# The down-projection of an MLP by quarters: seven block products in place of eight, with the block sums on GpSimd

## The reference

```python
def squared_relu_mlp(h, w_up, w_down):
    a = jax.nn.relu(h @ w_up)
    return (a * a) @ w_down

for layer in range(DEPTH):
    ...
    hn = rmsnorm(x, g[2])
    x = x + rmsnorm(squared_relu_mlp(hn, w_mlp_up[layer], w_mlp_down[layer]), g[3])
```

## Time and profile before

| | |
|---|---|
| median of 3 runs | 1166.92 us (1164.58 to 1167.45) |
| the profiled execution | 1166.92 us, its span 1165.1 us |
| mean granted TensorE clock | 0.985 of full speed |
| PE busy | 1116.0 us (96%) |
| DVE busy | 600.7 us (52%) |
| ACT busy | 450.2 us (39%) |
| POOL busy | 192.3 us (17%) |

### The profile page before, as it was taken

How to read it: one execution, slowest core, us unless ns; L and a number is a source line. 1 busy time by engine, 2 the same in 40 slices (tenths; PEclk the granted TensorE clock), 3 DMA queues, 4 the chain that set the end, 5 groups by cost and what they waited for, 6 DMA issues and landing times. The chain is left out here.

```text
span 1165.1 us, 15098 instructions
## 1 busy us (share of the span) xinstructions
PE 1116.0 (96%) x5577; PEld 896.5 (77%) x5577; DVE 600.7 (52%) x1106; ACT 450.2 (39%) x854; POOL 192.3 (17%) x338
## 2 busy tenths in 40 slices
PE   7999999999999999999899787999999999999997
PEld 6776678988888888888667665658988888888885
DVE  4353544543543643647377976634553453553554
ACT  6376554241321321335354366553332322322322
POOL 1354520000000000005303268340000000000004
PEclk9999899999999999999999889999999999999999
DMA  7431403354444344442423314003353543443431
GB/s 220 91 73 37 109 1 73 73 126 94 90 107 98 84 107 100 84 106 56 113 42 73 72 37 109 1 1 73 73 125 75 109 108 74 107 108 76 105 73 72
DMA packets 50782, 97.71 MB, mean 84 GB/s; under 512 B 4448, under 2 KB 4640, under 8 KB 50720
## 3 DMA queue, kind: packets, MB, share of 16 engines
q1 hardware_dynamic: 50208, 96.78, 36.5%
q10 hardware_dynamic: 512, 0.11, 0.1%
HBM read 94.78 MB, written 2.10 MB: 83 GB/s over the span
## 5 line engine op out<-in xcount | busy, mean ns | idle before, releaser
L1789 PE MATMUL bank<-w_hi,r_hi 128*128 128x512 f32 x512 | 199.3, 389 | 0.0
L1791 PE MATMUL bank<-w_hi,r_lo 128*128 128x512 f32 x512 | 199.2, 389 | 0.0
L1790 PE MATMUL bank<-w_lo,r_hi 128*128 128x512 f32 x512 | 199.2, 389 | 0.0
L1013 DVE SCALAR_TENSOR_TENSOR w_lo<-w_raw,gT,w_hi 128x512 fp32r<-128x512 f32 x152 | 104.5, 751 | 149.3 <-ACT w_hi L678 149.2
L1468 PE MATMUL bank<-r_hi,w_hi 128*128 128x512 f32 (+1 forms) x456 | 177.5, 389 | 0.0
L1469 PE MATMUL bank<-r_hi,w_lo 128*128 128x512 f32 (+1 forms) x456 | 177.4, 389 | 0.0
L1470 PE MATMUL bank<-r_lo,w_hi 128*128 128x512 f32 (+1 forms) x456 | 177.4, 389 | 0.0
L678 ACT ACTIVATE w_hi<-w_raw,gT 128x512 fp32r<-128x512 f32 x152 | 97.1, 713 | 174.7 <-PE bank L1791 103.7
L1003 DVE TENSOR_TENSOR w_lo<-w_raw,w_hi 128x2048 fp32r<-128x2048 f32 x34 | 78.3, 2302 | 124.7 <-ACT w_hi L670 124.7
L670 ACT ACTIVATE w_hi<-w_raw 128x2048 fp32r<-128x2048 f32 x36 | 68.9, 1913 | 157.5 <-PE bank L1791 118.7
L1790 PEld LDWEIGHTS bank<-w_lo,r_hi 128*128 128x128 f32 x512 | 96.1, 188 | 20.1
(11 more groups left out here) (169 smaller groups left out, 1664.7 us busy)
## 6 DMA issues: line engine op xcount, KB each, us to landing
w_raw<-in_w_mlp_up SPq DMA_DIRECT2D x64, 512.0 KB, 6.0
w_raw<-in_w_mlp_down SPq DMA_DIRECT2D x64, 512.0 KB, 6.4
w_raw<-in_b_w_in SPq DMA_DIRECT2D x16, 512.0 KB, 6.3
w_raw<-in_a_w_in SPq DMA_DIRECT2D x8, 512.0 KB, 6.7
w_raw<-in_a_w_out SPq DMA_DIRECT2D x8, 512.0 KB, 5.6
w_raw<-in_b_w_out SPq DMA_DIRECT2D x8, 512.0 KB, 5.9
X<-in_x SPq DMA_DIRECT2D x4, 512.0 KB, 6.7
w_raw<-in_a_w_in SPq DMA_DIRECT2D x8, 256.0 KB, 7.2
```

The lines of the kernel that those rows point to most:

```text
L1013: last = nc.vector.scalar_tensor_tensor(out=w_l[:, cs], in0=w_raw[:, slot, cs], scalar=g, in1=w_h[:, cs].bitcast(f32), op0=ALU.mult, op1=A ...
L1789: nc.tensor.matmul(bank[:], xh, hi[:, k, :], start=h == 0 and k == 0, stop=False)
L1790: nc.tensor.matmul(bank[:], xh, lo[:, k, :], start=False, stop=False)
L1791: ins = nc.tensor.matmul(bank[:], xl, hi[:, k, :], start=False, stop=h == 1 and k == 3)
```

## The change

Within a quarter the hidden activations A (512 tokens x 1024) and the down weights B (1024 x 1024) are cut into 2 x 2 blocks, A into blocks of 256 tokens x 512, B into blocks of 512 x 512. Seven products of Winograd's form of Strassen's method take the place of eight:

S1 = A21 + A22, S2 = S1 - A11, S3 = A11 - A21, S4 = A12 - S2; T1 = B12 - B11, T2 = B22 - T1, T3 = B22 - B12, T4 = T2 - B21.

They are numbered 0 to 6 in the order in which PE does them: A11 B11, S1 T1, S2 T2, S4 B22, A12 B21, S3 T3, A22 T4. Each is two token blocks x four hidden blocks x three matmuls, 24 matmuls of 512 columns. The products of the four quarters are added up each in an accumulator of its own (`acc`, seven of 2 x 512 a partition, read from the banks by DVE, `taken`), and only in the last quarter are the accumulators combined into the four blocks of y: six sums of 1024 on POOL (`total`), one on DVE, and the last two reads of banks go into y's blocks directly.

The eight sums of blocks S and T are made on POOL, each in two halves of 512 (S) or 1024 (T) numbers a partition, and written over blocks no longer needed. Up weights and B blocks now share four places for raw weights. High and low parts of the seven pairs are made in halves, on ACT (`a_high`, `b_high`) and DVE (`a_low`, `b_low`). ReLU is now on ACT (`relu_tile`), the square a product of ReLU and bank on DVE (`squared`). A product's weights take the two places of `w_hi` and `w_lo` in turn, so a place is free for product i when product i - 2 has left it. The quarters are written out in place of loops.

```diff
+PRODUCTS = (("A11", "B11"), ("S1", "T1"), ("S2", "T2"), ("S4", "B22"), ("A12", "B21"), ("S3", "T3"), ("A22", "T4"))
...
         @block.sync
...
+                for q in range(QUARTERS):
+                    u = u0 + MLP_UNITS * q
+                    if q == 0:
+                        for n in range(UPS):
+                            load(u + n, up_source(0, n))
+                        sp.wait_ge(x_new, 8 * (2 * layer + 1))
+                    else:
+
+                        sp.wait_ge(b_lo_done, part_no(layer, q - 1, 3, 1))
+                        sp.wait_ge(t_made, t_no(layer, q - 1, "T2", 1))
+                        fetch(u, up_source(q, 0))
...
+                        sp.wait_ge(*low_of(u))
+                    fetch((layer, q, "B22"), down_source(q, "B22"))
+                    sp.wait_ge(*low_of(u + (1 if q else 2)))
+                    fetch((layer, q, "B12"), down_source(q, "B12"))
+                    sp.wait_ge(*low_of(u + 3))
+                    fetch((layer, q, "B11"), down_source(q, "B11"))
+                    sp.wait_ge(b_lo_done, part_no(layer, q, 1, 1))
+                    sp.wait_ge(t_made, t_no(layer, q, "T2", 1))
+                    fetch((layer, q, "B21"), down_source(q, "B21"))
...
+            def weight_sum(layer, q, name, a):
...
+                elif name == "T1":
+                    pool.wait_ge(*loaded((layer, q, "B11")))
+                    pool.wait_ge(t_made, t_no(layer, q, "T3", a))
+                    nc.gpsimd.tensor_tensor(of("T1"), of("B12"), of("B11"), ALU.subtract).then_inc(t_made, 1)
+                elif name == "T2":
+                    pool.wait_ge(t_made, t_no(layer, q, "T1", a))
+                    pool.wait_ge(b_lo_done, part_no(layer, q, 0, a))
+                    nc.gpsimd.tensor_tensor(of("T2"), of("B22"), of("T1"), ALU.subtract).then_inc(t_made, 1)
...
+            def mlp(layer):
+                norm = 2 * layer + 2
+                for q in range(QUARTERS):
+                    last = q == QUARTERS - 1
+                    for a in range(2):
+                        weight_sum(layer, q, "T3", a)
+                    for a in range(2):
+                        hidden_sum(layer, q, "S3", a)
+                    for name in ("T1", "T2"):
+                        for a in range(2):
+                            weight_sum(layer, q, name, a)
+                    for name in ("S1", "S2", "S4"):
+                        for a in range(2):
+                            hidden_sum(layer, q, name, a)
+                    if last:
+                        pool.wait_ge(tile_out, part_tile(layer, q, 0, 1) + 1)
+                        total(layer, 2, 0, ALU.add)
+                        total(layer, 4, 0, ALU.add)
+                        pool.wait_ge(tile_out, part_tile(layer, q, 1, 1) + 1)
+                        total(layer, 3, 1, ALU.add)
+                    for a in range(2):
+                        weight_sum(layer, q, "T4", a)
+                pool.wait_ge(tile_out, part_tile(layer, QUARTERS - 1, 2, 1) + 1)
+                total(layer, 5, 2, ALU.add)
+                pool.wait_ge(acc_g, 6 * layer + 4)
+                total(layer, 1, 5, ALU.add)
+                total(layer, 6, 5, ALU.subtract)
+                gained(norm, 0, 1)
+                gained(norm, 1, 1)
...
         @block.vector
...
+            def a_low(layer, q, i, a):
+                hi, lo = (v[:, 2 * a:2 * a + 2, :] for v in hid[layer][A_PLACE[i]])
+                dve.wait_ge(a_hi_done, part_no(layer, q, i, a))
+                nc.vector.tensor_tensor(lo, a_of(PRODUCTS[i][0], a), hi.bitcast(f32), ALU.subtract).then_inc(a_lo_done, 1)
...
+                for q in range(QUARTERS):
...
+                    for i in range(2, PARTS):
+                        b_low(layer, q, i, 0)
+                        for j in range(2):
+                            taken(layer, q, i - 2, j)
+                        if last and i == 4:
+                            dve.wait_ge(acc_g, 6 * layer + 3)
+                            dve.wait_ge(tile_out, part_tile(layer, q, 2, 1) + 1)
+                            nc.vector.tensor_tensor(acc[:, 3], acc[:, 3], acc[:, 2], ALU.add).then_inc(acc_v, 1)
+                        b_low(layer, q, i, 1)
+                        for a in range(2):
+                            a_low(layer, q, i, a)
                     if not last:
...
+                        split(u + MLP_UNITS)
+                        for i in (5, 6):
+                            for j in range(2):
+                                taken(layer, q, i, j)
+                        split(u + MLP_UNITS + 1)
+                q = QUARTERS - 1
+                mean_square(norm, 0)
+                mean_square(norm, 1)
+                x_update(norm, 0)
+                x_update(norm, 1)
...
+                for j in range(2):
+                    taken(layer, q, 5, j)
+                for j in range(2):
+                    taken(layer, q, 6, j)
+                for j in range(2):
+                    last_gained(norm, 2 + j)
+                    mean_square(norm, 2 + j)
+                    x_update(norm, 2 + j)
...
         @block.tensor
...
+                def product(q, i):
+
+                    u = u0 + MLP_UNITS * q + UPS + i
+                    end = (q, i) == (QUARTERS - 1, PARTS - 1)
...
+                    order = [(k, j) for j in range(2) for k in range(4)] if end else [(k, j) for k in range(4) for j in range(2)]
+                    for k, j in order:
+                        t = MLP_TILES * q + 2 * UPS + 2 * i + j
+                        bank = banks[mlp_bank(layer, t)]
+                        if j == 0 and k % 2 == 0:
+                            pe.wait_ge(b_lo_done, part_no(layer, q, i, k // 2))
+                            pe.wait_ge(a_lo_done, part_no(layer, q, i, k // 2))
```

More of the change, by code:

```diff
@@ L637, in _ @@
                 x_squares(layer)
-            for j in range(NB):
-                gained(4, j, 0)
-            for j in range(NB):
-                if j < 3:
-                    gained(4, j, 1)
-                rstd_y(4, j)
+                mlp(layer)
         @block.scalar
@@ L673, in split @@
                         cs = slice(k * KI_COLS, (k + 1) * KI_COLS)
[L674 removed]
+                        last = nc.scalar.activation(w_h[:, cs], slot[:, cs], ACT.Copy, scale=gain(1, 0, k))
                 else:
@@ new lines, in mlp @@
+            def mlp(layer):
+                norm = 2 * layer + 2
+                for q in range(QUARTERS):
+                    last = q == QUARTERS - 1
+                    u = U[f"mlp{layer}"] + MLP_UNITS * q
+                    if q:
+                        split(u + 2)
+                    for t in range(4):
+                        relu_tile(layer, q, t)
+                    a_high(layer, q, 0)
+                    if q:
+                        split(u + 3)
+                    else:
@@ L851, in quarter @@
                         for j in range(NB):
                             x_square(2 * layer + 1, j)
-                    if last:
-                        sp(7)
-                        if not layer:
-                            split(U["qi"])
-                        for j in range(NB):
-                            y_square(2 * layer + 2, j, 0)
-                    else:
-                        for j in (7, 8, 9):
-                            sp(j)
-                quarter(0, False, first=True)
@@ new lines, in mlp @@
+                    if not last:
+                        split(u + MLP_UNITS)
+                        split(u + MLP_UNITS + 1)
+                if not layer:
+                    split(U["qi"])
+                for j, c in Y_ORDER[2:]:
+                    y_square(norm, j, c)
+                    if not layer and (j, c) == (1, 0):
+                        high(2, 0)
+                        split(U["qi"] + 1)
+                        high(2, 1)
+                        x_square(2, 0)
+                        x_square(2, 1)
@@ L980, in _ @@
             high(3, 3)
-            split(57)
-            split(58)
+            split(69)
+            split(70)
             mlp(1)
-            for j in range(NB):
-                y_square(4, j, 1)
         @block.vector
@@ new lines, in mlp @@
+                q = QUARTERS - 1
[3 more added lines that the diff above has]
+                x_update(norm, 1)
+                if not layer:
+                    low(norm, 0)
+                    split(U["qi"])
+                    low(norm, 1)
+                    split(U["qi"] + 1)
+                for j in range(2):
+                    taken(layer, q, 5, j)
+                for j in range(2):
+                    taken(layer, q, 6, j)
@@ L1297, in _ @@
+                for j in range(2):
+                    last_gained(norm, 2 + j)
+                    mean_square(norm, 2 + j)
+                    x_update(norm, 2 + j)
+                if not layer:
+                    low(norm, 2)
+                    q_low(1, 8)
+                    low(norm, 3)
```

(1 more changed line is left out.)

669 lines of the change are left out of this document (379 added, 290 removed).

## The result

After: 1249.05 us median of 4 executions (1248.18 to 1253.36). Before, on the same chip: 1166.6. The ratio is 1.0716, with a 95% interval from 1.0701 to 1.0731: slower by 7%, or 82 us. The forecast was 1238 in a range of 1186 to 1264.

The account below looks back on a forecast made before the run. TensorE's own work was taken to bound the MLPs. 1166.9 + 5.1 (first quarters) + 17.6 (middle) + 39.7 (last) + 9 (ends and between layers) = 1238 us, net of the saved matmuls; range 1186 to 1264.

Parts of the forecast that it names:

- What bounded the kernel: In the MLPs only TensorE's own work sets the time; 192 matmuls fewer at 0.2268 us remove 43.5 us.
- rival (a): No exclusion between GpSimd and VectorE: no product waits, only turns of 0.35 and the ends remain; 1128 us, chance 0.08.
- Exclusion in turns: VectorE splits and GpSimd sums, all inputs in SBUF, take turns; a middle quarter gets 4.4 us longer, four +17.6.
- Rival (b): Exclusion but better packed, VectorE using GpSimd's semaphore waits: about 1195 us, between 1186 and 1210, chance 0.22.
- B11's landing: In a middle quarter B11 lands 6.1 us after its fetch is issued, at 35.4 us; T1 and T2 hang on it.
- First quarters: B11 is there early, T1 done 13 us before product 0; stalls 2.4 + 5.25 + 0.35, so +2.6 each, +5.1.
- The clock under the waits: Stalls of 3 to 9 us lower TensorE's clock, 1.5 us lost each; in middle quarters absorbed by later waits, costed at nothing.
- rival (c): Two clock restarts a quarter, 1.5 us each, nothing absorbed: +24, 1262 us, chance 0.13.
- The full blocking: If the later of a GpSimd-VectorE pair waits for the first's end, turns cost 0.27 us more each: +25 us estimated.
- Last quarters: Accumulator sums and gains on GpSimd add turns in each layer's last quarter: stalls 25.3 less 5.44, +19.9 each, +39.7.
- The ends: Block-row updates and adds on VectorE after the last products: +4 us at the end, +5 between layers (0 to 8).
- rival (d): GpSimd sums of 1024 cost 3.3 us instead of the 2.40 taken: +54, 1292 us, chance 0.04.

Follow-up runs that it names:

- run 1: Changed kernel with every sum on GpSimd replaced by rows of small memsets that read nothing (output not the reference's): 1135.02 us, 0.9727 of the kernel before.
- run 4: Changed kernel with both hidden halves made ahead of the second weight half and the bank reads, on ScalarE and VectorE: 1256.3 us, 1.076.
- run 7: Changed kernel with all sums on VectorE, some in the up part, and B11 fetched a quarter early: 1162.4 us, 0.9955; timed again 1161.91, 0.9947.
- run 5: Changed kernel with B11 fetched a quarter ahead into a fifth raw place, except a layer's first, T1 and T2 in the up part: 1236.3 us, 1.0604.

## Why the prediction was right, and where its sizes were off

**What bounded the kernel.** Right: 192 records fewer, and in run 1, with nothing in the way, 31.6 us fewer of time. 43.5 less 2.1 of turns and 2.3 of ends was rival (a)'s 1128; 1135 was measured, 7 us more. They lie at the ends, not in the MLPs: between the layers run 1 is 6.4 us longer than the kernel before and at the end 3.2, where rival (a) had 1.3 and 1.0; its MLPs are 40.7 shorter, for 41.4, and its first down matmul comes 1.4 earlier.

**Exclusion in turns.** Right, and the core of it. T1 and T2 took 5.74 and 5.75 for two, against 5.7 and 5.7 of my turns; from the landing of B11, products 1, 2 and 3 started 16.5, 26.7 and 33.6 us later (429.77, 439.93 and 446.80 less 413.25), where the working had 16.5, 26.8 and 33.95. Rival (a) fell with the first half of T1. Rival (b) did too: the turns were packed as written down, and the one other order tried, in run 4, was no better.

**B11's landing.** The term that was mis-sized, and by a misreading. I took 6.1 us for the fetch from a median of 6.4; but those rows count transfers of 512 KB, and a block is two of them. In the kernel before, too, the two transfers of an MLP weight unit, issued 0.8 us apart, have both landed 7.3 us after the first was issued, at the median of its 64 such units. Here it took 7.5 (405.68 to 413.19): the first transfer landed 5.2 us after its issue, the second, issued 0.6 later, 6.9 after its own. Six quarters hang on it: 6 x 1.3 = 8 us of the 14 by which the MLPs were longer than forecast (76.8 for 62.4). Product 1's stall was 4.17 to 4.30 in these quarters, not 3.0.

**First quarters.** Their product 1 waited 3.54, not 2.4. My step was that T1 is done 13 us before product 0, since B11 is there early. It was done 0.6 before (POOL):

```profile
218.41 0.20 POOL L812 TENSOR_TENSOR small<-small 128x4 f32<-128x4 f32 x1 [28.84 <-ACT waste L927]
...
219.13 4.74 POOL L724 TENSOR_TENSOR w_raw<-w_raw,w_raw 128x1024 f32<-128x1024 f32 x2
223.83 3.53 POOL L697 TENSOR_TENSOR s<-hid_a 128x512 f32<-128x512 f32 x2
227.31 5.75 POOL L728 TENSOR_TENSOR w_raw<-w_raw 128x1024 f32<-128x1024 f32 x2
```

POOL's own queue held it: the small steps of the norm wait for ScalarE until 218.41, then T3 and S3 stand ahead of T1, and product 0 starts at 233.70. I had asked when the data are there, not when the engine gets to them. The two first quarters took 4.7 us more than the working for it: product 1 started 1.3 later in each, and product 3 another 1.2 and 0.9 after product 1.

**A turn that fell elsewhere.** Period 2 of layer 0 is 94.17 us, the others 92.6 to 92.9. There T4 ran ahead of a weight half (the DVE row at 346.19 lasts 3.42), product 2 started 2.2 us sooner after product 1, and product 3 waited 3.24 instead of 1.05. But it started 17.05 us after product 1, as in the next quarter (17.03): the turns add up to the same. What was lost is the clock behind the longer wait. Product 3 of this quarter and of the next:

```profile
352.60:359.80 7.20, 7.15 (x24) 5.78 (x25) 6.61 (x9) 1.06 (x1) 0.00 (x0) 0.76 0.86 200
446.80:452.40 5.60, 5.60 (x25) 4.62 (x26) 5.60 (x8) 2.21 (x4) 0.00 (x0) 1.00 0.85 191
```

The same 24 matmuls take 7.17 us at a granted clock of 0.76 and 5.56 at 1.00, and no wait for DVE stood behind them to take it up: 1.6 us that I had costed at nothing.

**The clock under the waits.** Right where a wait for DVE followed, which is the rule in middle quarters. Product 1 lasted from 429.77 to 438.11, 8.3 us instead of 5.44, and the idle time behind it was 1.82: together 4.7 of loss, for the forecast stall of 4.8. Product 2: 0.4 slower and 1.05 idle, 1.4 for 1.65. A slow clock ahead of a wait costs nothing, because the wait is for DVE. So rival (c), 24 us on top, did not come. What of it did is the 1.6 above and 0.3 to 0.4 in each of two quarters, where product 2 ran slow and no wait followed (253.01 and 1099.53: products 1 and 2 took 17.3 and 17.4 us instead of 17.0). The full blocking of which the Trainium skill (SBUF — State Buffer, Who interferes with whom) speaks would have added 25 us (an estimate from my sum). The rows show a little less than that: DVE's turns at 548.87 and 552.20 are 3.33 apart, less than 2.40 + 1.22 and as the working had it (2.27 + 1.07).

**Last quarters.** From product 1 to the last matmul 55.7 and 54.9 us, forecast 55.0. Inside, product 4 started 1.7 later than in the working, and by product 6 that was made up.

**The ends.** Between the layers +7.6 (forecast +5, bounds 0 and 8), at the end +2.4 (forecast +4). The last rows of DVE, which answer to the earlier trace rows: the four adds and the block rows behind them come as written down, with the last matmul at 1237.07.

```profile
1235.59 0.68 DVE L1508 TENSOR_TENSOR acc<-acc,bank 128x512 f32<-128x512 f32 x1
...
1244.56 0.74 DVE L1328 SCALAR_TENSOR_TENSOR X<-acc,small,X 128x512 f32<-128x512 f32 x1
```

**The head.** Not in the forecast: the first down matmul starts 4.2 us earlier than before. The windows show the granted clock between 100 and 150 us at 0.90 before and 0.97 after, in the same code. Much of it comes and goes in one and the same kernel: run 7's, traced twice, had its first down matmul at 233.49 with 0.97 there and at 236.04 with 0.93. So the sum is +76.8 in the MLPs, +7.6, +2.4 and -4.2: +82.6 of span, for a forecast of 71.5. That the total came out no further off is in part the head's doing, which the working did not have.

**Price of a 1024 sum.** 2.399 alone; rival (d) with 3.3 is out.

## What to carry to other kernels

An idle engine is not free capacity if it reads the memory that the busy one reads: moving the sums onto the engine that was already the busier one, with one block fetched earlier, took 87 us off. Add up the locked time of the pair, not the busy share of each, and look at the stretch after the last input becomes known, since nothing that is moved ahead of it shortens it. Saved matmuls are worth their time only when their operands' preparation fits below the products that remain; here the first kernel faster than before (run 7) had all sums on VectorE and a block fetched a quarter early, and no run tried the one without the other. Even then 4 to 10 us remained of the 43.5 saved.

## What the runs showed of the hardware

- Writes by GpSimd (memsets of 64 columns, 151 ns each) into the same memory left VectorE's two-input halves at 1.227 and 0.69 us (run 1); sums, which read two inputs there, stretched them to 1.90 and 1.80 at the mean.
- In turns neither engine starves: with work queued on both, a pair of 1024 comes back every 3.33 us.
- VectorE's sum of 1024 takes 1.22, GpSimd's 2.40; of 512, 0.69 and 1.3 (the rows of L496 in runs 7 and 5).
- In the changed kernel's down products the first matmul after a wait of 3.18 to 9.68 us lasted 0.76 to 0.77 us in 9 of 13 places and 0.47 in the others; after a wait of 0.62 to 2.86 us it lasted 0.47 in all 12; the stretch from 550 to 560 us, with 10 us of almost no work, was granted 0.57.
- One kernel can take one of two times 5 us apart with nothing changed but the mean granted clock (run 7's kernel, 0.98 or about 0.974); in the two traced executions 2.5 us of it lie ahead of the first down matmul of layer 0 (233.49 and 236.04).
- Two transfers of 512 KB issued 0.6 to 0.8 us apart have both landed 7.3 to 7.5 us after the first was issued (medians of 64 pairs each), where the median of one is 6.0 to 6.6.
